# Softmax steps right behind their scores, two products in turns behind a normalization, and two rotations in the halves of one bank

## The reference, cut to what matters

```python
def rmsnorm_2(x, g):
    y = xf * lax.rsqrt(jnp.mean(xf * xf, axis=-1, keepdims=True) + EPS) * g

def swiglu(h, w1, w3, w2):
    return (jax.nn.silu(h @ w1) * (h @ w3)) @ w2

def memory_branch(mq, gate, mem_n, w_mem_kv):
    s = einsum('bshd,bmhd->bhsm', q, k) * (MEM_DH ** -0.5)
    p = jax.nn.softmax(s, axis=-1)
    return einsum('bhsm,bmhd->bshd', p, v) * jax.nn.silu(gate)

def rotary(t):                     # q and k of the retention layer
    return concatenate([t1 * cos - t2 * sin, t1 * sin + t2 * cos], axis=-1)

def dilated_group(q, k, v, dil, span):     # three groups per head, one joint softmax over them
    s = where(mask, einsum(q, k) * D ** -0.5, -1e30)
```

## Time and profile before

| | us |
|---|---|
| median of 3 runs | 4209.85 (4208.52 to 4211.24) |
| the profiled execution, own time | 4205.0 |
| its span, first to last instruction | 4203.1 |
| TensorE busy in the span | 3915.5 (93%) |
| DVE, ACT, POOL busy | 1749.6, 1598.6, 1359.3 |
| mean granted TensorE clock | 0.971 |

### The profile page before, as it was taken

How to read it: one execution, slowest core, us unless ns; L and a number is a source line. 1 busy time by engine, 2 the same in 40 slices (tenths; PEclk the granted TensorE clock), 3 DMA queues, 4 the chain that set the end, 5 groups by cost and what they waited for, 6 DMA issues and landing times.

```text
span 4203.1 us, 81850 instructions
## 1 busy us (share of the span) xinstructions
PE 3915.5 (93%) x35588; PEld 3368.2 (80%) x35588; DVE 1749.6 (42%) x2271; ACT 1598.6 (38%) x2022; POOL 1359.3 (32%) x632
## 2 busy tenths in 40 slices
PE   8999999899998899999998999997899999999988
PEld 5776777788886788888886788886788888888887
DVE  2242216566655544443444344435333333333333
ACT  3342225512213444443444343434344444444433
POOL 2331113100002344444443344443333333333333
PEclk9999999999998999999998999998999999999999
DMA  8887664100002455555553454454555555555544
GB/s 324 282 295 254 232 222 156 42 4 4 4 10 105 153 188 187 185 188 185 185 175 120 149 173 148 161 170 126 173 176 168 161 160 163 168 161 161 161 136 140
DMA packets 183123, 667.52 MB, mean 159 GB/s; under 512 B 20432, under 2 KB 20432, under 8 KB 182384
## 3 DMA queue, kind: packets, MB, share of 16 engines
q1 hardware_dynamic: 176544, 642.07, 46.7%
q10 hardware_dynamic: 4944, 16.03, 1.1%
q0 software_dynamic: 1280, 4.20, 0.2%
HBM read 653.82 MB, written 8.39 MB: 158 GB/s over the span
## 4 chain that ended last, share of the span: by engine, by line
PE 84%; DVE 7%; ACT 4%; issue 2%; DMA 2%; POOL 1%; PEld 0%; ACTq 0%; POOLq 0%; PEldq 0%; DVEq 0%; SPq 0%
PE ps L973 66%; PE ps L925 2%; PE ps L1190 2%; PE ps L1214 2%; PE ps L1126 2%; PE ps L1204 1%; ACT whl L1440 1%; DVE xw L1930 1%; DVE tm L1927 1%; ACT work L1440 1%; DVE whl L1924 1%; POOL whl L2504 1%; PE ps L1412 1%; PE ps L1428 1%; ACT xw L1440 1%
## 5 line engine op out<-in xcount | busy, mean ns | idle before, releaser
L973 PE MATMUL ps<-halves,whl 128*128 128x256 f32 (+1 forms) x14752 | 2624.7, 338 | 81.5 <-DVE halves L1924 16.1
L973 PEld LDWEIGHTS ps<-halves,whl 128*128 128x128 f32 x14752 | 2261.0, 192 | 412.7 <-issue 87.1
L2504 POOL TENSOR_TENSOR whl<-raw,whl 128x1024 fp32r<-128x1024 f32 x508 | 1240.2, 2442 | 2002.6 <-ACT whl L1440 2002.4
L1440 ACT ACTIVATE whl<-raw 128x1024 fp32r<-128x1024 f32 x1016 | 1064.8, 1055 | 1291.5 <-PE ps L973 931.8
L1924 DVE TENSOR_TENSOR whl<-raw,whl 128x1024 fp32r<-128x1024 f32 x508 | 755.1, 1487 | 1496.3 <-ACT whl L1440 1496.2
L973 PE MATMUL ps<-whl,halves 128*128 128x256 f32 x2752 | 495.9, 339 | 0.3 <-POOL whl L2504 0.3
L973 PEld LDWEIGHTS ps<-whl,halves 128*128 128x128 f32 x2752 | 423.6, 192 | 64.2 <-issue 9.4
L1440 ACT ACTIVATE work<-ps 128x512 f32<-128x512 f32 (+1 forms) x240 | 131.6, 550 | 345.5 <-PE ps L973 274.2
L2504 POOL TENSOR_TENSOR halves<-mix,halves 128x1024 fp32r<-128x1024 f32 (+1 forms) x16 | 28.6, 1795 | 550.7 <-ACT halves L1440 550.7
L1924 DVE TENSOR_TENSOR work<-work,ps 128x512 f32<-128x512 f32 x157 | 107.8, 686 | 159.0 <-ACT work L1440 159.0
L925 PE MATMUL ps<-raw,sc 128*32 128x256 f32 x1536 | 113.8, 393 | 3.4 <-DMA raw<-in_ada 3.3
(11 more groups left out here) (247 smaller groups left out, 2465.4 us busy)
## 6 DMA issues: line engine op xcount, KB each, us to landing
raw<-in_ffn SPq DMA_DIRECT2D x264, 512.0 KB, 4.2
raw<-in_ada SPq DMA_DIRECT2D x192, 512.0 KB, 4.7
raw<-in_w_kv SPq DMA_DIRECT2D x192, 512.0 KB, 3.5
raw<-in_w_in_b SPq DMA_DIRECT2D x160, 512.0 KB, 4.0
raw<-in_w_in_a SPq DMA_DIRECT2D x128, 512.0 KB, 3.7
raw<-in_mem SPq DMA_DIRECT2D x64, 512.0 KB, 5.4
raw<-in_w_out_a SPq DMA_DIRECT2D x48, 512.0 KB, 3.9
raw<-in_w_out_b SPq DMA_DIRECT2D x48, 512.0 KB, 3.6
```

The source lines that it names most:

```text
L973: p = self.e.matmul(o, x, y, start=bi not in begun, stop=final and kc == 3 and m == len(pairs) - 1, skip_group_check=True)
L1440: return self.e.activation(out, in_, func, **kw)
L2504: return self.e.tensor_tensor(out, a, b, op)
```

## The change

Four things are done. (1) In `mem_head` and `dil_head` DVE's softmax and ACT's exponentials are put into the queues in the step of the scores; the memory head's two halves share one maximum and one reciprocal instruction. (2) Before the feed-forward part, layer A and layer B five slices of the normalization are issued, and then two products take turns tile by tile with two slices behind each (`beside`); the stream has the same order. In layer B the kv normalization is taken up two slices a step beside the later groups. The fences ahead of the layers move in front of the normalizations. (3) The step counts change: 3 tiles a step in layer A, 2 in the memory groups of layer B. (4) In the retention stage the two rotations of a tile go into the halves of bank 7 and are issued behind the second tile; DVE waits for both.

```diff
--- before.py
+++ after.py
@@ -76,13 +76,19 @@
     add("w_out", range(4), range(2))
     add("w_out", range(4), range(2, 4))
     add("w_out", range(4, 8))
+    def in_turns(name_a, a, name_b, b):
+        names.extend(t for kg in range(4) for t in ((name_a, a, kg), (name_b, b, kg)))
+
     for k0, k1 in ((0, 4), (4, 8), (8, 11)):
-        for j in range(2 * k0, 2 * k1):
+        if k0 == 0:
+            in_turns("ffn1", 0, "ffn3", 0)
+        for j in range(max(1, 2 * k0), 2 * k1):
             add("ffn1", [j])
             add("ffn3", [j])
         for n in range(8):
             add("ffn2", [n], range(k0, k1))
-    for h in range(4):
+    in_turns("w_in_a", 24, "w_in_a", 28)
+    for h in range(1, 4):
         add("w_in_a", [24 + h, 28 + h])
     for p in range(4):
         add("w_in_a", [p, 4 + p, 8 + 2 * p, 16 + 2 * p, 9 + 2 * p, 17 + 2 * p])
@@ -92,7 +98,8 @@
         add(name, range(4, 8), EARLY + (3,))
 
     begun("w_out_a")
-    for h in range(4):
+    in_turns("w_in_b", 32, "w_in_b", 36)
+    for h in range(1, 4):
         add("w_in_b", [32 + h, 36 + h])
     for p in range(8):
         add("w_in_b", [p, 8 + p, 16 + p])
@@ -360,27 +367,28 @@
         for g in outs:
             rest(g)
         self.root_of_sums(3)
-        rest(self.normed(3, 3, "HA"))
         for part, (k0, k1) in enumerate(((0, 4), (4, 8), (8, 11))):
             for j in range(2 * k0, 2 * k1):
-                rest(self.gemm("ffn1", j, range(4), self.halved("B", "HA"), "v", lambda g, j=j: self.glu_gate(g, j)))
-                rest(self.gemm("ffn3", j, range(4), self.halved("B", "HA"), "v", lambda g, j=j, k0=k0: self.swiglu(g, j, 2 * (j - 2 * k0))))
+                gate = self.gemm("ffn1", j, range(4), self.halved("B", "HA"), "v", lambda g, j=j: self.glu_gate(g, j))
+                value = self.gemm("ffn3", j, range(4), self.halved("B", "HA"), "v", lambda g, j=j, k0=k0: self.swiglu(g, j, 2 * (j - 2 * k0)))
+                if j:
+                    rest(chain(gate, value))
+                else:
+                    self.beside(self.normed(3, 3, "HA"), gate, value)
             for n in range(8):
                 rest(self.gemm("ffn2", n, range(k0, k1), self.halved("B", "HB"), "v2",
                                lambda j, n=n, part=part: self.ev_x(j, n, 5, 4 if part == 2 else None), kbase=k0))
         self.root_of_sums(4)
         self.norm_in_place(0, 4)
         self.rms(5, 0, 0)
-        rest(self.normed(4, 5, "HA"))
         self.f4 = self.fence()
         self.begin_retention()
         self.m2, self.heads_begun, self.ring, self.ring_name = 0, 0, self.w2, "w"
-        heads = self.pipeline(self.memory_groups(0, "w_in_a", 24) + self.retention_groups(), 2)
+        heads = self.pipeline(self.memory_groups(0, "w_in_a", 24) + self.retention_groups(), 3, self.normed(4, 5, "HA"))
         self.project("w_out_a", 0, 6, heads, 3)
         self.root_of_sums(6)
-        rest(self.normed(5, 6, "HA"))
         self.f6 = self.fence()
-        rest(self.pipeline(self.memory_groups(1, "w_in_b", 32), 3, self.normed(6, 6, "HB")))
+        rest(self.pipeline(self.memory_groups(1, "w_in_b", 32), 2, self.normed(5, 6, "HA"), self.normed(6, 6, "HB")))
         self.f8 = self.fence()
         self.begin_dilated()
         heads = self.pipeline_tight(self.dilated_groups())
@@ -454,6 +462,11 @@
 
     def rope_bank(self, R):
         return 6 if R < 2 else 2 + R % 2 if R < 10 else 7
+
+    def rope_out(self, R):
+
+        at = T * (R % 2) if R >= 10 else 0
+        return self.G(self.rope_bank(R))[:, at:at + T]
 
     def ada_tile(self, t):
         pass
@@ -710,8 +723,8 @@
 
     def then_rotate(self, g):
 
-        for _ in g:
-            if self.turns:
+        for i, _ in enumerate(g):
+            if i == 1 and self.turns:
                 self.rotate(*self.turns.pop())
             yield
 
@@ -746,18 +759,24 @@
 
         self.freed[self.ring_name, m] = (name, key)
 
-    def pipeline(self, groups, ratio, before=None):
+    def beside(self, normed, a, b):
+
+        rest(limited(normed, 5))
+        run_all((alternate(a, b), 1), (normed, 2))
+
+    def pipeline(self, groups, ratio, normed, later=iter(())):
+
+        heads = None
         for tiles, after in groups:
-            def products(ts):
-                for _, g in ts:
-                    yield from g
             made = tiles()
-            if before is None:
-                rest(products(made))
+            if heads is None:
+                for _, g in made[:2]:
+                    rest(g)
+                self.beside(normed, made[2][1], made[3][1])
             else:
-                run_all((products(made), ratio), (before, 1))
-            before = after([m for m, _ in made])
-        return before
+                run_all((chain(*[g for _, g in made]), ratio), (heads, 1), (later, 2))
+            heads = after([m for m, _ in made])
+        return heads
 
     def pipeline_tight(self, groups):
         before = None
@@ -976,9 +995,12 @@
 
     def rope_product(self, R, raw, rot):
         b = self.rope_bank(R)
-        self.bank(b, "rope_v", (R, "sin"))
+        if R < 10:
+            self.bank(b, "rope_v", (R, "sin"))
+        elif R % 2 == 0:
+            self.bank(b, "rope_v", (R + 1, "sin"))
         self.wait_ge(*raw)
-        self.e.matmul(self.G(b)[:, 0:256], rot, self.tm[R % 4], start=True, stop=True).then_inc(self.sig("rope_mm", R), 1)
+        self.e.matmul(self.rope_out(R), rot, self.tm[R % 4], start=True, stop=True).then_inc(self.sig("rope_mm", R), 1)
 
     def ev_kA(self, job):
         for fb in range(2):
@@ -1859,13 +1881,13 @@
         self.big_freed[slot] = ("mh_mm", (h, "o"))
         self.wait_ge("mh_mm", (h, "s"))
         self.act(p[:, 0:512], self.X(0), ACT.Copy).then_inc(self.sig("mh_s", (h, "p")), 1)
-        yield
+        k = 8 * (h % 8)
+        self.wait_ge("mh_v", (h, "nm"))
         for qb in range(2):
-            k = 8 * qb + 4 * (ch % 4)
             pq = p[:, 256 * qb:256 * qb + 256]
-            self.wait_ge("mh_v", (h, qb, "nm"))
-            self.act(pq, pq, ACT.Exp, bias=self.cols[:, k + 1:k + 2], scale=1.0 / 16,
-                     accum_out=self.cols[:, k + 2:k + 3]).then_inc(self.sig("mh_s", (h, qb, "e")), 1)
+            self.act(pq, pq, ACT.Exp, bias=self.cols[:, k + 2 + qb:k + 3 + qb], scale=1.0 / 16,
+                     accum_out=self.cols[:, k + 4 + qb:k + 5 + qb]).then_inc(self.sig("mh_s", (h, qb, "e")), 1)
+        yield
         self.wait_ge("mh_mm", (h, "t"))
         self.act(p[:, 0:512], self.X(1), ACT.Copy).then_inc(self.sig("mh_s", (h, "pt")), 1)
         yield
@@ -2049,9 +2071,9 @@
 
     def rope_rest(self, R, dst, sin):
         raw = self.tm[R % 4]
-        self.wait_ge("rope_mm", R)
+        self.wait_ge("rope_mm", R if R < 10 else R | 1)
         self.wait_ge("rope_g", R)
-        self.tt(raw, self.G(self.rope_bank(R))[:, 0:256], sin, MUL).then_inc(self.sig("rope_v", (R, "sin")), 1)
+        self.tt(raw, self.rope_out(R), sin, MUL).then_inc(self.sig("rope_v", (R, "sin")), 1)
         self.wait_ge("rope_v", (R, "sin"))
         self.tt(dst, dst, raw, ADD).then_inc(self.sig("rope_v", (R, "add")), 1)
 
@@ -2439,10 +2461,19 @@
         slot = self.heads_begun % 2
         self.heads_begun += 1
         p, g = self.big[slot], self.ring[mg % len(self.ring)]
-        yield
+        k = 8 * (h % 8)
+        mx, nm, rs = (self.cols[:, k + 2 * i:k + 2 * i + 2] for i in range(3))
         self.wait_ge("mh_s", (h, "p"))
+        self.e.tensor_reduce(mx, p[:, 0:512].rearrange("p (q n) -> p q n", q=2), AX.X, MAX).then_inc(self.sig("mh_v", (h, "mx")), 1)
+        self.wait_ge("mh_v", (h, "mx"))
+        self.ts1(nm, mx, -1.0 / 16, None, MUL).then_inc(self.sig("mh_v", (h, "nm")), 1)
+        self.wait_ge("mh_s", (h, 1, "e"))
+        self.e.reciprocal(rs, rs).then_inc(self.sig("mh_v", (h, "rc")), 1)
+        self.wait_ge("mh_v", (h, "rc"))
         for qb in range(2):
-            self.softmax_rows("mh_v", (h, qb), "mh_s", p[:, 256 * qb:256 * qb + 256], 8 * qb + 4 * (ch % 4), 1.0 / 16)
+            pq = p[:, 256 * qb:256 * qb + 256]
+            self.ts1(pq, pq, rs[:, qb:qb + 1], None, MUL).then_inc(self.sig("mh_v", (h, qb, "p")), 1)
+        yield
         yield
         self.wait_ge("mh_mm", (h, "o"))
         for s in self.tok[mg]:
```

8 lines of the change are left out of this document (4 added, 4 removed).

## The result

The changed kernel takes 4052.95 us (median of 4 runs, 4049.6 to 4056.5). The kernel before took 4209.19 beside it (4 runs, 4199.57 to 4211.24). The ratio is 0.9633, with a 95% interval of 0.9616 to 0.9651: 156 us less, where 139 were forecast. In a second set of runs, beside other kernels, the changed kernel took 4052.71 and the kernel before 4198.4, ratio 0.9651 (0.9629 to 0.9674). The profiled execution took 4049.6 us, with a span of 4047.8, which is 155.3 us less than the span before.

A forecast was written before the change was run, and what follows sets the result against it. TensorE, busy 93% of the span, was taken as the bound, so only its idle and slow time could be won. Gains of 66 + 18 + 23 + 20 + 12 = 139 us from 4205.0 gave 4066, 4071 as a median; range 4050 to 4115.

The forecast's parts named there:

- dilated stage and projection: Dilated heads, 28 softmaxes and 4 in the projection: early softmax removes 55 us of waits, 11 slow time; 66, bounds 34-66.
- memory heads A: Layer A's memory heads: early softmax removes 12.7 us of waits and 5.9 of slow time; 18 us, bounds 12 and 19.
- rotations: Retention stage: issuing both products together removes 16.5 us of waits and 6.2 of slow time; 23 us, bounds 15 and 24.
- three normalizations: Ahead of feed-forward, layers A and B: eight tiles in 24.8 us; gains 5.7, 7.0, 7.7, together 20, bounds 5 and 22.
- memory heads B: Layer B's memory heads: 29.7 us of hole, waits and slow time become 17.9; gain 12 us, bounds 5 and 20.
- a price at each of the 28 waits: Dilated stage: slow time counted behind every wait would win 36 us more; the forecast kept 8.1 from the rows.
- its own sign, under 26: Behind each normalization: eight tiles taking under 26 us would show the prediction right.
- rival (b): Products after a normalization starve as ACT's split waits for a product before slices; 15 us less gain, 4086; chance 0.07.
- The splits' slack: ACT's split behind a softmax: held about 3.6 us against 4.6 to spare (5.5 where DVE subtracts), so nothing booked.
- (c): Retention stage: rotations still wait, the first product now for its input; 23 us less gain, 4094; chance 0.04.
- (d): Slow time in dilated, projection, layer A and rotations isn't due to waits and stays; 23 less, 4094; chance 0.06.
- (e): Slower: a late split delays the refill and is never made up over 40 softmaxes; 4247 us; chance 0.03.

The follow-up runs named there:

- again: A second profile of the same kernel, unchanged, taken of the kernel before (span 4203.7 us) and of the changed kernel (median 4052.71 us).
- the two other orders tried: Changed kernel with three kv normalization steps beside two products in layer B (4054.72 us), and with three steps beside three products (4063.6 us).

## Why the prediction was right, and where by luck

From the profiled spans, before to after, in its own terms (forecast, measured):

| term | forecast | measured | from |
|---|---|---|---|
| dilated stage and projection | 66 | 66.6 | dilated stage 1011.75 to 960.76; P to end 15.6 |
| memory heads A and rotations | 18 + 23 | 43.1 | A to B 49.1, less 6.0 for the normalization |
| three normalizations | 20 | 14.2 | 30.5 to 27.0, 33.0 to 27.0 less 0.9 of later start, 32.5 to 26.9 |
| memory heads B | 12 | 12.4 | 159.12 to 141.17, less 5.6 |
| sum | 139 | 136.3 | |
| not in the sum | 0 | 19.0 | 12.9 level of the feed-forward stage, 6.05 ahead of F |

The sum was right to 3 us, and for the reasons given: waits and the slow time behind them are two terms, and both went. So close a fit is partly the choice of profiles: the first row would be 74.2 from the second pair (again), since the dilated stage took 1013.8 and 955.7 us there.

In the dilated stage the first pair gave 44.1 of waits and, net, 6.9 more. Its first 624 products took 111.8 us in after and 108.4 in before, so 3.4 were lost there to a slow start and the slow level, and the slow time won behind the waits is 10.3, where 8.1 had been taken. The rows were the better guide than a price at each of the 28 waits, 36 us more. The Trainium skill has the half clock as the default that only activity lifts ("TensorE: Matmul & The Clock Gate", section "What's actually happening").

**Rotations.** The term was 23, and alone they gave 26.1. The count was one slip, eight waits of 17.6 us, not seven of 16.5; the slow time was the other, 8.5 where 6.2 had been taken.

**Normalizations.** This term was mis-sized: 24.8 us for eight tiles, measured 26.1 to 26.3 and 0.6 to 0.9 of a pause behind them, and its own sign, under 26, didn't come. The prediction gave DVE four slices (3.2 us) and a split (1.2 to 1.5) for every two tiles, under 5 us in all; in the feed-forward stage they took 6.7 to 6.8, since one step in them takes 2.4 beside POOL in place of 0.48 and 0.35 is a wait for ACT. The rule of the shared port pair was weighed, but for the softmax multiplies of layer B, where it would have cost 7 us. Two of them take 0.61 us together there (2842.34), so they paid nothing. It bore on the term one section earlier instead, and in layer B on DVE's splits, of which one takes 2.54 us beside POOL (2827.41), not 1.23. The 5.8 us that are missing are within the 15 of rival (b), but its mechanism, ACT held up by a split that waits for a product, is not what the rows show.

**Memory heads B.** 12 against 12.4 is two errors that cancel. The wait that came back was 9.05 + 2.2 at the second head, where 6 + 1.8 at the third was written; the 1.9 of a fourth tile and the small waits didn't come. The cause given was the last four or five slices ahead of a softmax. The trace has six, two to a row, between the gate tile's last step and the maximum:

```profile
2834.24 0.88 DVE L1949 SCALAR_TENSOR_TENSOR tm<-x,const,rst 128x256 f32<-128x256 f32 x2
...
2840.08 0.69 DVE L2467 TENSOR_REDUCE cols<-work 128x2 f32<-128x512 f32 x1 [1.25 <-ACT work L1462]
```

Taking them three at a turn doesn't help, and spreading them over three groups does: there were too many in one.

**The splits' slack.** Behind a wide softmax in the dilated stage stands a split that DVE subtracts, with 5.8 us to spare (the prediction had 5.5 for that kind), and it is held for 3.1. The prediction set its hold of 3.6 against 4.6, the kind with less, so booking nothing was right with more room than stated. Rivals (c), (d) and (e) had nothing in the traces.

**The 19.0 outside the sum.** The forecast took every stage without an edit as fixed. The measured 4052.95 lies only 3 us above the lower end of the range, 4050; by this pair of profiles it would be some 4072 without the 19.0, next to the forecast's 4071. The spread of the kernel before, 4190.49 to 4218.83 over all sets, which were measured after the forecast, says that single executions differ by more than 10 us, in such stages too; the three that the forecast had, 4208.52 to 4211.24, didn't show it. With the median of before between 4198.4 and 4209.19 from set to set, the change is worth 146 to 156 us, and the forecast's 139 is somewhat low for either end.

## What to carry to other kernels

When an engine at 93% waits for a softmax, look at what is queued ahead of the softmax on its engines, and emit the chain right behind its input; then work out what it holds up, for the engine that subtracts that tile's split and not for the worst one. Elementwise work that is to hide beside products needs its amount compared with the products of that stretch, hand-overs included: in the two other orders tried the wait inside the stretch only moved, while spreading it over three stretches took 9.9 us out. And compare the stages that an edit doesn't touch, in at least two profiles of each kernel, before a difference in them is given to the edit.

## What the runs showed of the hardware that was not expected

- A stretch of matmuls without a pause runs at one of two levels, 173.4 or 176.7 ns a matmul in this mix, at a granted clock of 1.00 in both. The level can change across a pause of 1.5 us, and across other matmuls without a pause; within a stretch it wasn't seen to change. Two executions of one program had different levels in the same stretch (192 matmuls in 34.08 and 33.44 us).
- 1.9% of TensorE's rate over 700 us is 12.9 us, nearly as much as the three normalizations gave, and no busy share and no clock shows it: only the count of matmuls in equal windows does.
- A DVE step of 0.48 us took 2.38 beside a POOL subtraction of 2.39, and ended 0.28 us behind it. A DVE multiply of 128x768 took 1.79 us beside POOL's split and 0.62 away from it.
